# Two-layer mixture-of-experts network on Trainium2: the second expert's projection set ahead of the spreading of the choices, the first weighing and the meta rows

## The reference, cut to what matters

```python
def hierarchical_moe(h, w_group, b_group, w_expert, b_expert, w_gate, w_up, w_down):
    ...
    g = jnp.argmax(glog, axis=-1)              # one of 4 groups for each token
    ...
    vals, loc = lax.top_k(elog_g, TOP_K)       # two of its 8 experts
    gates = pg * jax.nn.softmax(vals, axis=-1)
    ...
    def expert_block(args):
        xb, e = args
        hb = jax.nn.silu(xb @ w_gate[e]) * (xb @ w_up[e])
        return hb @ w_down[e]
    ...
    y = jnp.zeros((T + 1, D), x2.dtype).at[slot_tok].add(ys * slot_gate[:, None])
    return y[:T].reshape(Bsz, S, D)

for i in range(DEPTH):                         # first block, DEPTH = 2
    mixed = rglru_mixer(h, ...) if i % 2 == 0 else shortconv_mixer(h, ...)
    h = layer_norm(ALPHA * h + mixed, ...)
    h = layer_norm(ALPHA * h + hierarchical_moe(h, ...), ...)
return h[:, N_META:]
```

## Time and profile before

| what | value |
|---|---|
| runs of the kernel before | median 1856.42 us of 3 runs, 1854.1 to 1859.62 |
| profiled execution | 1853.74 us, its span 1852.0 us |
| mean granted clock of TensorE in it | 0.914 of full |
| expert stage of layer 0, about | 141 to 600 us of the span |
| expert stage of layer 1, about | 747 to 1199 us of the span |
| moved by DMA | 540.28 MB, 292 GB/s over the span |
| busy over the span | PE 85%, DVE 41%, ACT 12%, POOL 4% |
| all projections of experts (L805) | 304.4 us busy, 206.8 us idle before them |

### The profile page before, as it was taken

The page is one execution under the profiler, slowest core; times in us unless marked ns, Lnnn a source line. Parts: engine busy times, 40 slices in busy tenths (PEclk is TensorE's granted clock), DMA queues, the critical chain, the costliest instruction groups (busy, mean ns, idle before and its releaser), DMA issues. The chain is left out here.

```text
span 1852.0 us, 31977 instructions
## 1 busy us (share of the span) xinstructions
PE 1571.7 (85%) x14321; PEld 1030.5 (56%) x14321; DVE 757.8 (41%) x1575; ACT 229.0 (12%) x562; POOL 75.8 (4%) x95
## 2 busy tenths in 40 slices
PE   8999868889877899795756656689999999999998
PEld 6654534455444885452423333378699545769843
DVE  5753233532124313322311111270467653657756
ACT  2311111101111000110211000111000003400000
POOL 2000100000000100000000000060000001000000
PEclk9999978988888899997878777799999999999999
DMA  9477999999998849699999999946535434325420
GB/s 333 151 286 296 419 382 426 423 425 424 424 425 343 339 157 373 275 418 425 422 425 422 421 424 416 378 148 228 176 143 183 163 106 162 137 91 188 177 91 23
DMA packets 88118, 540.28 MB, mean 292 GB/s; under 512 B 7374, under 2 KB 9486, under 8 KB 54188
## 3 DMA queue, kind: packets, MB, share of 16 engines
q1 hardware_dynamic: 86092, 531.24, 71.6%
q0 software_dynamic: 1888, 6.95, 1.0%
HBM read 531.89 MB, written 6.29 MB: 291 GB/s over the span
## 5 line engine op out<-in xcount | busy, mean ns | idle before, releaser
L805 PE MATMUL ps<-ring,work 128*32 128x256 f32 x3968 | 304.4, 470 | 206.8 <-DMA ring<-in_moe_w_up 196.1
L805 PEld LDWEIGHTS ps<-ring,work 128*32 128x32 f32 x3968 | 159.0, 130 | 335.5 <-issue 267.1
L2197 DVE TENSOR_TENSOR rowb<-rowb,ps 128x128 f32<-128x128 f32 x64 | 18.4, 287 | 374.5 <-ACT rowb L1611 374.5
L2203 DVE COPY multi<-ps 128x256 f32<-128x256 f32 x64 | 27.2, 424 | 257.6 <-PE ps L818 257.6
L818 PE MATMUL ps<-ring,multi 128*32 128x256 f32 x1920 | 118.9, 390 | 1.3 <-ACT multi L1616 0.7
L756 PE MATMUL ps<-hT,ring 128*128 128x258 f32 (+2 forms) x528 | 118.9, 387 | 0.0
L1329 PE MATMUL ps<-ring,work 128*128 128x512 f32 x256 | 114.5, 593 | 0.0
L782 PE MATMUL ps<-ring,work 128*128 128x512 f32 x256 | 110.9, 593 | 0.0
L756 PEld LDWEIGHTS ps<-hT,ring 128*128 128x128 f32 x528 | 100.0, 190 | 18.6 <-issue 2.5
L1294 PE MATMUL ps<-hT,ring 128*128 128x128 f32 x768 | 95.5, 276 | 1.5 <-ACT hT L1517 1.5
L1294 PEld LDWEIGHTS ps<-hT,ring 128*128 128x128 f32 x768 | 90.4, 192 | 2.0 <-ACT hT L1517 2.0
(11 more groups left out here) (509 smaller groups left out, 1948.9 us busy)
## 6 DMA issues: line engine op xcount, KB each, us to landing
ring<-in_moe_w_gate SPq DMA_DIRECT2D x62, 2048.0 KB, 18.7
ring<-in_moe_w_up SPq DMA_DIRECT2D x62, 2048.0 KB, 23.2
ring<-in_moe_w_down SPq DMA_DIRECT2D x60, 2048.0 KB, 23.2
ring<-in_w_ff SPq DMA_DIRECT2D x32, 2048.0 KB, 8.2
ring<-in_sc_w_in SPq DMA_DIRECT2D x6, 2048.0 KB, 17.8
ring<-in_ssm_w_glu SPq DMA_DIRECT2D x4, 2048.0 KB, 19.0
ring<-in_lru_w_in SPq DMA_DIRECT2D x3, 2048.0 KB, 14.5
ring<-in_lru_w_out SPq DMA_DIRECT2D x2, 2048.0 KB, 23.6
```

Of the source, the lines that this page charges most:

```text
L805: mm = pe.matmul(ps[32 * q:32 * q + 32, bank, 0:256].rearrange("p (u n) -> p u n", u=2), x[:, k % 2, k // 2, :], gu[:, k, :, 2 * P * (q // ...
L2197: V.tensor_tensor(hid[b], silu[b], ps[:, 4 + b, P:2 * P], ALU.mult).then_inc(S(f"hid_ready{l}"), 1)
L2203: V.tensor_copy(y_out[b], ps[:, 4 + b, 0:256]).then_inc(S(f"y_ready{l}"), 1)
```

## The change

Step 0 loses the spreading and the meta rows; the spreading moves behind projection 1, the first weighing behind `down` of expert 1, the meta rows to step 3 (`META_AT`). The picking of expert 1's rows now comes right behind projection 0, ahead of the choices' transposes, and the turning of those rows ahead of `down` of expert 0. The choices' transposes go to PSUM bank 7 in place of 5, and wait for `rounds_known`. In DVE's list `slot_weights` of expert 0 and 1 both stand in step 1, behind the product of expert 1 and ahead of the copy of its result. `pick_rows` has a wait for the `xT` that the picked rows' bank held before, which `turn_rows` had. The wait for `spread_out` on PE moves from ahead of `value_load` to ahead of `weigh_in(0)`. The same numbers of matmuls, copies and DMAs are issued as before. No DMA is added, taken away or put in another order.

```diff
--- before.py
+++ after.py
@@ -46,6 +46,7 @@
 NGRP = NE // GROUP
 EXTRA = 5
 EARLY = 2
+META_AT = 3
 KEEP_AT = (4, 5)
 CHUNK = 4
 NCH = SEQ // CHUNK
@@ -960,11 +961,11 @@
                 def turn_choices():
 
                     pe.wait_ge(*nth(f"choices_ready{l}", 1))
-                    pe.wait_ge(*nth(f"xT_ready{l}", 2))
+                    pe.wait_ge(*nth(f"rounds_known{l}", 1))
                     for i, b in enumerate(blocks):
                         m = BLOCKS[b][1]
                         at = BLOCKS[b][0] - (0 if l == 0 else NMETA)
-                        mm = pe.transpose(ps[0:4, 5, at:at + m], choices[0:m, i, :], ident[0:m, 0:m])
+                        mm = pe.transpose(ps[0:4, 7, at:at + m], choices[0:m, i, :], ident[0:m, 0:m])
                     mm.then_inc(S(f"choices_turned{l}"), 1)
 
                 def spread_choices():
@@ -1004,27 +1005,29 @@
                         gate_up(xT[0], 4, gu, range(0, DC, 2))
                         pe.wait_ge(*nth(f"xT_ready{l}", 2))
                         gate_up(xT[0], 4, gu, range(1, DC, 2)).then_inc(S(f"gate_up{l}"), 1)
+                        pe.wait_ge(*nth(f"one_hots{l}", 2))
+                        pick_rows(l, blocks, 1)
                         turn_choices()
                     else:
                         gate_up(xT[b], 4 + b, gu).then_inc(S(f"gate_up{l}"), 1)
                     if e == 1:
-                        pe.wait_ge(*nth(f"spread_out{l}", 1))
-                        pe.wait_ge(*nth(f"rounds_known{l}", 1))
+                        spread_choices()
                         rounds = pe.value_load(rounds_i[0:1, l:l + 1], min_val=1, max_val=MAX_ROUNDS)
-                    if e >= 1:
+                    if e >= 2:
                         weigh_in(e - 1)
                     if e in KEEP_AT:
                         keep_rows(KEEP_AT.index(e) + 1)
                     pe.wait_ge(*nth(f"hid_ready{l}", e + 1))
                     pe.transpose(ps[:, 4 + b, 256:256 + P], hid[b], ident[:, :]).then_inc(S(f"hid_turned{l}"), 1)
                     if e == 0:
-                        spread_choices()
-                    if e + 1 < NE:
+                        turn_rows(l, 1)
+                    elif e + 1 < NE:
                         pe.wait_ge(*nth(f"one_hots{l}", (e + 1) // GROUP + 2))
-                        if l == 0 and e >= 1:
+                        if l == 0 and e > META_AT:
                             pe.wait_ge(*nth("meta_out", 1))
                             if preps:
                                 pe.wait_ge(*nth("prep_out", preps))
+                        pe.wait_ge(*nth(f"xT_ready{l}", e + 2))
                         pick_rows(l, blocks, e + 1)
                     pe.wait_ge(*nth(f"hidT_ready{l}", e + 1))
                     if e == EARLY:
@@ -1037,12 +1040,14 @@
                         pe.wait_ge(loaded[down_], (expert_turn[l, e, "down"] + 1) * 16)
                         last = halves_of(ring[:, down_, :])
                     down(hidT[b], 4 + b, last).then_inc(S(f"down{l}"), 1)
-                    if e + 1 < NE:
-                        pe.wait_ge(*nth(f"xT_ready{l}", e + 2))
+                    if e == 1:
+                        pe.wait_ge(*nth(f"spread_out{l}", 1))
+                        weigh_in(0)
+                    if 1 <= e and e + 1 < NE:
                         turn_rows(l, e + 1)
-                    if l == 0 and e == 0:
+                    if l == 0 and e == META_AT:
                         pe.wait_ge(*nth("meta_rows", 1))
-                        pe.wait_ge(*nth("xT_ready0", 3))
+                        pe.wait_ge(*nth("xT_ready0", META_AT + 3))
                         for c in range(DC):
                             mm = pe.transpose(ps[:, 6, NMETA * c:NMETA * c + NMETA], meta_rows[:, P * c:P * c + P], ident[0:NMETA, 0:NMETA])
                         mm.then_inc(S("meta_turned"), 1)
@@ -1610,18 +1615,20 @@
                     act.wait_ge(*nth(f"gate_up{l}", e + 1))
                     A(silu[b], ps[:, 4 + b, 0:P], ACT.Silu).then_inc(S(f"silu{l}"), 1)
                     if e == 0:
+                        rows_kept(1)
                         act.wait_ge(*nth(f"choices_turned{l}", 1))
-                        A(flat[:, 0:nt], ps[0:4, 5, 0:nt], ACT.Copy).then_inc(S(f"choices_flat{l}"), 1)
+                        A(flat[:, 0:nt], ps[0:4, 7, 0:nt], ACT.Copy).then_inc(S(f"choices_flat{l}"), 1)
                     act.wait_ge(*nth(f"hid_turned{l}", e + 1))
                     A(hidT[b], ps[:, 4 + b, 256:256 + P], ACT.Copy).then_inc(S(f"hidT_ready{l}"), 1)
-                    if e == 0:
+                    if e == 1:
                         act.wait_ge(*nth(f"choices_spread{l}", 1))
                         A(spread[:, :, 0:nt], ps[:, 0:4, 0:nt], ACT.Copy).then_inc(S(f"spread_out{l}"), 1)
                     if e + 1 < NE:
-                        rows_kept(e + 1)
+                        if e >= 1:
+                            rows_kept(e + 1)
                         act.wait_ge(*nth(f"dispatched{l}", e + 2))
                         A(xT[(e + 1) % 2], turned, ACT.Copy).then_inc(S(f"xT_ready{l}"), 1)
-                    if l == 0 and e == 0:
+                    if l == 0 and e == META_AT:
                         act.wait_ge(*nth("meta_turned", 1))
                         A(meta_h[:, :, :], ps[:, 6, 0:DC * NMETA].rearrange("p (c t) -> p c t", c=DC), ACT.Copy).then_inc(S("meta_out"), 1)
                     if l == 0:
@@ -2189,21 +2196,21 @@
                 route(l)
                 for e in range(NE):
                     b = e % 2
-                    if e >= 1:
+                    if e >= 2:
                         slot_weights(l, e)
                     if e % GROUP == GROUP - 1 and e + 1 < NE:
                         next_one_hots(l, (e + 1) // GROUP)
                     dve.wait_ge(*nth(f"silu{l}", e + 1))
                     V.tensor_tensor(hid[b], silu[b], ps[:, 4 + b, P:2 * P], ALU.mult).then_inc(S(f"hid_ready{l}"), 1)
-                    if e == 0:
+                    if e == 1:
                         dve.wait_ge(*nth(f"spread_out{l}", 1))
-                        dve.wait_ge(*nth(f"rounds_known{l}", 1))
-                        slot_weights(l, 0)
+                        for first in range(2):
+                            slot_weights(l, first)
                     dve.wait_ge(*nth(f"down{l}", e + 1))
                     V.tensor_copy(y_out[b], ps[:, 4 + b, 0:256]).then_inc(S(f"y_ready{l}"), 1)
                     if e == 1:
                         link(V.tensor_scalar(alphas, ident[:, :], ALPHA, None, ALU.mult))
-                    if l == 0 and e == 0:
+                    if l == 0 and e == META_AT:
                         V.tensor_copy(two(meta_rows, DC), unpacked(hres[0:NMETA, 0, :])).then_inc(S("meta_rows"), 1)
                     if l == 0:
                         s5_constants(e)
```

## The result

| | runs | median, us | span of the profiled execution | mean granted clock in it |
|---|---|---|---|---|
| before | 7 | 1855.6 (1853.51 to 1859.62) | 1852.0 | 0.914 |
| after | 7 | 1846.22 (1842.91 to 1850.25) | 1846.4 | 0.916 |

The ratio is 0.9949, with a 95% interval of 0.9934 to 0.9964.

The account below looks back on a forecast made before the run. The weight stream was taken to bound both expert stages, with holes where it waits for TensorE. Gains of 4.0 us (layer 0) and 1.8 (layer 1) sum to 5.8, so 1856.42 becomes 1850.6 us; range 1846.5 to 1855.5.

Parts of the forecast that it names:

- What bounds the kernel, and the mechanism: Both expert stages: the weight stream bounds; holes wait for TensorE's first steps, so earlier releases fill 4.3 and 4.7 us.
- the release is 4.0 us earlier, out of a hole of 4.3: Layer 0: projection 1 ends at 157.1 instead of 161.1, releasing expert 3's gate load 4.0 us earlier.
- I leave that stretch where it is: Layer 0, 150 to 154 us: some 3.4 us at half clock assumed to stay, ahead of projection 1's end.
- a second stretch: Rival, chance 0.17: another half-clock stretch on projection 1; layer 0 gains 2.3, sum 4.1, time 1852.3 us.
- Layer 1, 1.8 us: Layer 1: expert 3's down load, released by `down` of expert 1, goes out 1.8 us earlier and the hole shrinks equally.
- The moved work: Later steps: moved weighing, spreading and meta rows are covered; layer 0's projection 2 ends at 169.1, with cover of 2.5 us.
- 146.9, which doesn't move: Layer 0: end of projection 0, taken as the fixed starting point of the walk to the release.
- The sum: Whole kernel: 4.0 us from layer 0 plus 1.8 from layer 1 gives 5.8.
- The 1.7 us from release to data: Layer 0's hole: stream restarts 1.7 us behind the releasing projection, said to disagree with the skill's 0.6 us.
- the stream dry at expert 8: Rival, chance 0.12: layer 0, PE's lead is eaten; layer 0 keeps 2.0, sum 3.8, time 1852.6 us.
- a late projection 2: Slower rival, chance 0.05: step 1 chain delays layer 0's projection 2 past 171.6, each microsecond costing one; 1862.1 at 14.
- does little: Rival, chance 0.12: earlier releases, but `down` behind the spreading and the clock take gains back; some 2 us left, 1854.4.

Follow-up runs that it names:

- The doses: dose_release and dose_narrow: the changed kernel with extra pickings in layer 0; 1850.27 and 1849.51 us.
- the layers alone: l0_only and l1_only: the new order in one layer, the old order in the other; 1848.5 and 1851.44 us.
- the meta rows: Two runs: the old order with only the meta rows moved to step 3, 1850.58 us; the changed kernel with them back in step 0, 1847.99 us.
- before_again: The kernel before, unedited, run once more against itself; 1853.65 us, ratio 1.0001.
- l1_only: The new order in layer 1 alone, the old order and meta rows in step 0 in layer 0; 1851.44 us, ratio 0.9986 to the kernel before.
- after_again: The changed kernel, unedited, run once more; 1846.36 us, ratio 0.996 to the kernel before.
- l0_only: The new order in layer 0 alone, with the meta rows in step 3, the old order in layer 1; 1848.5 us, ratio 0.9964 to the kernel before.
- meta_at_0: The changed kernel with the meta rows back in step 0; 1847.99 us, ratio 0.9965 to the kernel before.
- dose_release: The changed kernel with three more pickings of expert 1's rows ahead of projection 1 in layer 0; 1850.27 us, ratio 0.998 to the kernel before.
- dose_narrow: The changed kernel with five more pickings in step 5 of layer 0; 1849.51 us, ratio 0.9983 to the kernel before.
- the larger comparison: The later batch with more runs, changed kernel against kernel before; 7.4 us faster by the ratio, 7.0 by the means (35 runs of the kernel before).

## Why the prediction was wrong

**What bounds the kernel, and the mechanism: right.** The doses, the layers alone and the meta rows all follow distance, hole, length.

**Layer 0, "the release is 4.0 us earlier, out of a hole of 4.3": mis-sized.** This is the step that failed, in two places. The larger is the hole, which caps the gain. It was read from one trace; in the other two of the three traces of the whole old order it was 5.9, those with the second stretch, and the mean is 5.4. The smaller is "I leave that stretch where it is". No trace of the new order with the meta rows away had a half-clock stretch ahead of the release; where one came in the first steps, it came behind the spreading, which now stands behind the release. Projection 1 ended 8.2 us behind projection 0, where the forecast has 157.1 - 146.9 = 10.2: 1.6 of the 2.0 are the stretch, the rest are smaller waits than I allowed. The hole closed entirely, which in the prediction's own trace is worth 4.3 in place of 4.0. Lengths give 445.8 - 440.5 = **5.3 us** (means of before, before_again, l1_only and of after, after_again, l0_only). I had priced a second stretch as a danger for the new order; it was one of the old, and never seen in the new with the meta rows away.

**Layer 1, 1.8 us: mis-sized the other way.** Projection 1 ended 7.4 us behind projection 0, for 7.9 foretold. But the moved spreading brought the half clock onto picking and `down` of expert 1 (1.49 and 3.25 for 1.07 and 1.91): 6.6 us to the end of `down`, for 4.9. The down load went out only 0.5 us earlier (13.97 for 14.46). Where the stretch didn't come (meta_at_0, dose_release, dose_narrow) it was 2.2. The length fell by 1.5 all the same, 437.2 (mean of before, before_again and l0_only) to 435.7. The earlier release gives 0.5 of it; the rest would be smaller holes at later loads. The three lengths of the old order differ by 3.1 among themselves, so that the rest is not shown to be the change's.

**The moved work: right.** The first weighing waited for nobody and started at 163.87, right behind `down`. The prediction's "146.9, which doesn't move" did move, to 148.46, by what came ahead of the stage. Counted from there, projection 2 ended 21.7 us on, where 169.1 - 146.9 = 22.2 was foretold and 24.7 allowed; the slow picking and `down` ate part of what the earlier projection 1 had won. The meta rows waited their 1.31 us in step 3, and projection 4 started 38.8 us on, for 39.3 foretold. No hole at 172 or 218 us.

**The sum.** 5.3 + 1.5 = 6.8 us by the lengths of the streams, for 5.8. The two profiled executions differ by 5.6, which fits the forecast by accident: before's was the old order's luckier case. The means of all runs give 7.0 in the larger comparison and the ratio 7.4 [4.8 to 10.0]; the first comparison's 9.4 [6.7 to 12.2] holds both, and what lies above 7 in it no run explains. **The range** had room for 6.1 us of gain and 3.8 of noise below 1856.42. The result lies 10.2 below that: 0.8 because the kernel before itself came out at 1855.6, 6.8 by the streams, and 2.6 that stay open. With the 6.8 alone it would have been 1848.8, inside the range, so the 1.0 us missing from the forecast doesn't by itself explain why the time fell out of it. In the larger comparison the changed kernel's median was 1846.36 again, and 1.9 of the same distance were the kernel before (1854.54): the median of three runs that the prediction started from lay above both later ones.

**The lag and the clock.** The 1.7 us from release to data stayed: by the windows of layer 1 the load issued at 764.52 counts as flowing at 425 GB/s from about 766.2 on. But this is not the time to the first data. In narrower windows of the changed kernel the first data show 1.0 to 1.2 us behind that issue:

```profile
764.50:765.00 0.50, 0.50 (x12) 0.48 (x16) 0.47 (x2) 0.00 (x0) 0.00 (x0) 1.00 0.00 0
765.00:765.50 0.50, 0.50 (x13) 0.17 (x5) 0.09 (x1) 0.00 (x0) 0.00 (x0) 1.00 0.00 0
765.50:765.75 0.25, 0.25 (x6) 0.16 (x2) 0.05 (x1) 0.00 (x0) 0.00 (x0) 1.00 2.55 393
```

The issue itself takes 0.38 us, so the first data come some 0.6 to 0.85 us behind its end. The page "DMA: Bandwidth & Descriptors" of the Trainium skill, section "Latency and other measured facts", has about 0.6 to the first byte; the trace is near it, and the prediction set two different quantities side by side when it said that they disagree. For the hole the 1.7 is the one that counts. The page "TensorE: Matmul & The Clock Gate" of the Trainium skill, section "What's actually happening", says that activity lifts the clock; by it I had put the denser order's gain at 4.3 in layer 0, and the denser order did run its way to the release at full clock. But the half clock behind the spreading came while PE had been busy without a break (2.00 of 2 us in the windows at 156 and 158), which by itself no rule of busy against idle foretells.

**Rivals.** A second stretch on projection 1, the stream dry at expert 8 and a late projection 2 didn't occur; "does little" is excluded by both comparisons.

## What to carry to other kernels

When a stage is bound by a stream of loads, look for windows in which the stream stands still, and walk back from the issue that ends each: what the engine does ahead of that release is worth its full time, and the same work behind it is free while the next release has reserve. Move from that path first whatever brings a wait or a low clock with it (the meta rows' 0.67 us of transposes cost 3 to 4), and check that the issue order doesn't tie a load to a later release than it needs: gate first in layer 1 made its stream 4.8 us shorter for one line. Take the size of a hole from several traces, since one trace's clock is one draw.
